# The low part of the SwiGLU and convolution weight tiles: GpSimd in place of VectorE

## The reference

```python
h = modulate(rmsnorm(x, norm_ffn[i]), sh2, sc2)
x = x + g2 * ((silu(h @ w_gate) * (h @ w_up)) @ w_down)      # D_FF = 2816
b, c, v = split(h @ w_in); y = (b * conv3(c * v)) @ w_out    # layer 1's mixer
```

## Time and profile before

| | |
|---|---|
| median of the runs | 2868.98 us |
| span of the profiled execution | 2866.1 us |
| TensorE matmuls, share of the span | 90% |
| VectorE | 1353.8 us, 47% |
| ScalarE | 672.1 us, 23% |
| GpSimd | 343.2 us, 12% |
| mean granted TensorE clock | 0.945 |
| `w_lo` on VectorE | 172 instructions, 203.1 us |

### The profile page before, as it was taken

One profiled execution on the slowest core, in us unless ns is written; L12 is line 12 of the kernel. 1 busy time (PEld: TensorE's weight loads), 2 busy tenths in 40 slices (PEclk: granted clock), 3 DMA queues, 4 the chain that ended last, 5 costly groups with the idle time before them and its releaser, 6 DMA issues.

```text
span 2866.1 us, 30876 instructions
## 1 busy us (share of the span) xinstructions
PE 2585.1 (90%) x11501; PEld 2104.4 (73%) x11501; DVE 1353.8 (47%) x1995; ACT 672.1 (23%) x993; POOL 343.2 (12%) x241
## 2 busy tenths in 40 slices
PE   8658888888796999999999969999969999999997
PEld 8546667676584888888788747877748888888886
DVE  0645666666584444444444444334443334444334
ACT  2323444444433111111111231111221111111111
POOL 3322222222105000000000140000140000000002
PEclk9878999999997999999999969999969999999998
DMA  6000111111320222222222201111101111111101
GB/s 238 28 6 23 36 35 35 35 35 35 118 96 1 81 76 93 74 79 73 88 80 73 96 30 45 37 59 37 44 1 58 44 44 59 44 44 53 50 29 59
DMA packets 47978, 162.67 MB, mean 57 GB/s; under 512 B 5152, under 2 KB 6560, under 8 KB 47776
## 3 DMA queue, kind: packets, MB, share of 16 engines
q1 hardware_dynamic: 47904, 161.72, 16.6%
HBM read 157.51 MB, written 4.19 MB: 56 GB/s over the span
## 4 chain that ended last, share of the span: by engine, by line
PE 77%; DVE 7%; issue 7%; POOL 5%; ACT 3%; DMA 1%; DVEq 0%; ACTq 0%; SPq 0%; POOLq 0%
PE ps L315 23%; PE ps L316 22%; PE ps L317 22%; POOL tmp L1497 3%; POOL acc L1488 2%; PE ps L624 2%; PE ps L580 1%; PE ps L581 1%; PE ps L584 1%; PE ps L582 1%; ACT pbuf L921 1%; PE ps L585 1%; DVE w_lo L1094 1%; PE ps L494 1%; DVE pt_lo L1094 1%
## 5 line engine op out<-in xcount | busy, mean ns | idle before, releaser
L315 PE MATMUL ps<-h_hi,w_hi 128*128 128x512 f32 x1792 | 715.3, 399 | 78.1 <-DVE h_lo L1094 78.0
L316 PE MATMUL ps<-h_lo,w_hi 128*128 128x512 f32 x1792 | 708.1, 395 | 0.0
L317 PE MATMUL ps<-h_hi,w_lo 128*128 128x512 f32 x1792 | 707.9, 395 | 0.0
L315 PEld LDWEIGHTS ps<-h_hi,w_hi 128*128 128x128 f32 x1792 | 341.4, 191 | 173.8 <-DVE h_lo L1094 103.3
L1296 DVE SCALAR_TENSOR_TENSOR x<-ps,mods,x 128x512 f32<-128x512 f32 x480 | 350.2, 749 | 206.0 <-PE ps L317 204.5
L315 PE MATMUL ps<-g_hi,w_hi 128*128 128x512 f32 x960 | 382.1, 398 | 39.5 <-DVE x L1296 34.2
L317 PEld LDWEIGHTS ps<-h_hi,w_lo 128*128 128x128 f32 x1792 | 342.9, 191 | 72.6
L316 PEld LDWEIGHTS ps<-h_lo,w_hi 128*128 128x128 f32 x1792 | 343.3, 192 | 68.8
L316 PE MATMUL ps<-g_lo,w_hi 128*128 128x512 f32 x960 | 378.6, 394 | 0.0
L317 PE MATMUL ps<-g_hi,w_lo 128*128 128x512 f32 x960 | 377.9, 394 | 0.0
L1353 DVE TENSOR_TENSOR ab<-ab,ps 128x512 f32<-128x512 f32 x88 | 60.5, 688 | 634.6 <-PE ps L317 633.0
(11 more groups left out here) (168 smaller groups left out, 2703.0 us busy)
## 6 DMA issues: line engine op xcount, KB each, us to landing
raw<-stream SPq DMA_DIRECT2D x176, 512.0 KB, 4.2
mod_raw_f<-ada_rows SPq DMA_DIRECT2D x48, 512.0 KB, 3.4
mod_raw<-ada_rows SPq DMA_DIRECT2D x32, 512.0 KB, 3.5
ada_ring<-ada_pe SPq DMA_DIRECT2D x16, 512.0 KB, 13.0
x<-x_t SPq DMA_DIRECT2D x2, 2048.0 KB, 15.7
x<-x_t SPq DMA_DIRECT2D x8, 512.0 KB, 6.4
out_t<-x SPq DMA_DIRECT2D x16, 256.0 KB, 2.1
hraw<-head_w SPq DMA_DIRECT2D x8, 384.0 KB, 3.9
```

Of the source, the lines that this page charges most:

```text
L315: nc.tensor.matmul(out, w[0][wi], a[0][ai], start=start, stop=False)
L316: nc.tensor.matmul(out, w[0][wi], a[1][ai], start=False, stop=False)
L317: return nc.tensor.matmul(out, w[1][wi], a[0][ai], start=False, stop=stop)
```

## The change

From the first SwiGLU on, GpSimd makes every `w_lo`. VectorE's calls of `tile_lo` in `ffn_block`, `conv_block` and `turn` go, and GpSimd gets loops over the same tiles in the same order, with a wait for ScalarE's cast ahead of each. In the turn after the first SwiGLU the two down tiles come between GpSimd's multiplications for the two halves; in every phase GpSimd's tiles of the last block stand ahead of its sums of squares. Which tiles, buffers and slots are used, and what ScalarE, TensorE and SyncE do, stays. The 18 tiles made before the first SwiGLU stay on VectorE.

```diff
-        def ffn_block(blk, prefetch, mod_count, out_at, gate):
+        def ffn_block(blk, mod_count, out_at, gate):
             for f in range(2):
                 for half in range(2):
                     ffn_inner(blk, f, half)
                     share = mod_count // 4
                     mod_rows((2 * f + half) * share, (2 * f + half + 1) * share)
-                if prefetch:
-                    for k in range(2):
-                        tile_lo(w_lo[:, 2 * f + k, :], w_hi[:, 2 * f + k, :], k)
...
-                if prefetch:
-                    down_tiles()
...
         def conv_block(blk, col, gate):
-            for k in range(2):
-                tile_lo(w_lo[:, 6 + k, :], w_hi[:, 6 + k, :], k)
             for f in range(2):
...
                 conv_inner(blk, f, lambda tap: taps[:, tap:tap + 1])
-                for k in range(3):
-                    tile_lo(w_lo[:, 3 * f + k, :], w_hi[:, 3 * f + k, :], (3 * f + k) % 2)
...
+        def tile_lo(slot, k):
+
+            C.add("t_hi")
+            pool.wait_ge(t_hi, C.at("t_hi"))
+            nc.gpsimd.tensor_tensor(w_lo[:, slot, :], raw[k][:], w_hi[:, slot, :].bitcast(F32), ALU.subtract)\
+                .then_inc(t_lo, 1)
...
+        for p, (kind, blocks, _, _) in enumerate(PHASES[1:], 1):
+            if kind == "ffn":
+                with pool.Fori(0, blocks - 1) as i:
+                    C.enter(i, {"t_hi": 6})
+                    for k in range(6):
+                        tile_lo(k, k % 2)
+                    C.leave(blocks - 1)
+                if p < 3:
+                    for k in range(4):
+                        tile_lo(k, k % 2)
+            else:
+                with pool.Fori(0, blocks) as i:
+                    C.enter(i, {"t_hi": 8})
+                    for k in (6, 7, 0, 1, 2, 3, 4, 5):
+                        tile_lo(k, k % 2)
+                    C.leave(blocks)
+            if p < 3:
+                turn(p, down_tiles if kind == "ffn" else (lambda: None))
```

More of the change, by code:

```diff
@@ L1367, in mod_rows @@
                 C.add("mod_used")
-        def down_tiles():
-            for k in range(2):
-                tile_lo(w_lo[:, 4 + k, :], w_hi[:, 4 + k, :], k)
-        def ffn_block(blk, prefetch, mod_count, out_at, gate):
+        def ffn_block(blk, mod_count, out_at, gate):
             for f in range(2):
@@ L1435, in _ @@
             if kind == "ffn":
-                per = {"sil": 4, "pj": 8, "gm": 4, "t_hi": 6, "v": 4}
+                per = {"sil": 4, "pj": 8, "gm": 4, "v": 4}
                 if n_mod:
@@ L1440, in _ @@
                     C.enter(i, per)
-                    ffn_block(i + first_blk, True, n_mod, i * 4 + (N_PE_MOD + N_ATT_MOD), gate)
+                    ffn_block(i + first_blk, n_mod, i * 4 + (N_PE_MOD + N_ATT_MOD), gate)
                     C.leave(blocks - 1)
-                ffn_block(last, p < 3, 2 * n_mod, N_PE_MOD + N_ATT_MOD + n_mod * (blocks - 1), None)
+                ffn_block(last, 2 * n_mod, N_PE_MOD + N_ATT_MOD + n_mod * (blocks - 1), None)
             else:
@@ L1446, in _ @@
                 with dve.Fori(0, blocks - 1) as i:
-                    C.enter(i, {"t_hi": 8, "cs": 8, "zm": 4, "pj": 12, "v": 16})
+                    C.enter(i, {"cs": 8, "zm": 4, "pj": 12, "v": 16})
                     conv_block(i + first_blk, i * 6, gate)
@@ L1455, in _ @@
             if p < 3:
-                turn(last, job, gate, down_tiles if kind == "ffn" else (lambda: None))
+                turn(last, job, gate, lambda: None)
             else:
@@ L1562, in _, with turn @@
             group(gb, True)
-        for p in range(4):
+        def tile_lo(slot, k):
[3 more added lines that the diff above has]
+                .then_inc(t_lo, 1)
+        def turn(p, tail):
             j = J_MIX + 2 * p
@@ L1568, in _ @@
                 add_squares(j, m, HT)
[L1569 to L1572, removed]
             add_squares(j + 1, 1, HT)
@@ L1577, in _, with down_tiles @@
                     add_squares(j + 1, k + 2, HT)
+            tail()
             for k in range(KD):
                 mul_rstd(j + 1, x[:, k, HALF[1]], HT)
+        def down_tiles():
+            for k in range(2):
+                tile_lo(4 + k, k)
+        turn(0, lambda: None)
+        C.n["t_hi"] = PRO_TILES + N_OUT_TILES
+        pool.wait_ge(t_lo, PRO_TILES + N_OUT_TILES)
+        for p, (kind, blocks, _, _) in enumerate(PHASES[1:], 1):
[16 more added lines that the diff above has]
+                turn(p, down_tiles if kind == "ffn" else (lambda: None))
+        for j in (J_MIX + 6, J_MIX + 7):
+            for m in range(1, KD):
+                add_squares(j, m, HT)
 def kernel(x, c, ctx, c_ctx, ada_w, ada_b, norm_mix, norm_ffn, mla_w_dq, mla_q_norm, mla_w_uq, mla_w_dkv,
```

## The result

The kernel after takes 2904.99 us (median of 4 runs, 2903.16 to 2905.55), beside 2868.36 us for the kernel before on the same chip: 1.0131 times as long, with an interval of 1.0117 to 1.0146. The change costs 36.6 us where I had forecast 25. The sign, the places and nearly all the mechanisms are those of the forecast; the size of the clock's loss in the first SwiGLU is not, and the two turns lose more than it had.

The account below looks back on a forecast made before the run. TensorE, 90% busy, was taken as the bound, VectorE mattering only where TensorE waits for to_x. 22 + 20 + 2.2 + 1.1 - 20.3 = +25.0 on a span of 2866.1, plus 2.9 for the median: 2894.0 us, range 2861 to 2908.

Parts of the forecast that it names:

- One tile on GpSimd: A w_lo subtraction of 128x1024 on GpSimd takes 2.36 us, where VectorE needs 1.2.
- The port: VectorE and GpSimd share SBUF access; a blocked instruction waits for the other's whole instruction; to_x, reading PSUM, isn't held.
- a row product that isn't held: Faster rival, first SwiGLU: the row product passes beside GpSimd, -8 us, 2861 (2851 if the copy passes too); chance 0.17.
- The chain: First SwiGLU: VectorE's work from last up product (t) to to_x grows 2.2 us in ten blocks, +22 us.
- The clock: First SwiGLU: TensorE's clock halves after waits of 3.1 us, 2.0 us in each of ten blocks, +20 us.
- The last block: First SwiGLU's last block: two row products in the slot, to_x at 1636.2 for 1634.02, +2.2 us.
- The turn after it: Turn after the first SwiGLU: GpSimd's down tiles block the first of VectorE's diagonal scalings, +1.1 us.
- the 2 us that I had named as a sign: Sign in the turn after the first SwiGLU: diagonal scalings of about 2 us.
- The convolution: Convolution: to_x no longer waits for the third tile's load; three blocks regain 6.8 us each, -20.3 us.
- The fourth block: Convolution's last block: TensorE waits for GpSimd's sums in place of to_x; 0, between -1.3 and +1.4 us.
- The second SwiGLU: Second SwiGLU: g_lo ends at t + 4.0 and to_x follows, against t + 4.1 before; 0.
- the slowest rival: GpSimd keeps the port for both tiles; second SwiGLU waits too, convolution regains half: +50 us, 2919; chance 0.07.

Follow-up runs that it names:

- experiment 3: The kernel after with each GpSimd w_lo tile made by two instructions of 128x512: 2869.27 us, 1.0007 of the kernel before.
- experiment 7: The kernel after with the fourth row product of each looped first-SwiGLU block replaced by a one-column copy: 2869.83 us, 1.001 of the kernel before.
- experiment 6: The kernel before, all w_lo on VectorE, with tiles TensorE doesn't need yet moved behind the first two or eight to_x: 2834.47 us, 0.9889.
- experiment 4: The kernel before with two extra VectorE tile subtractions in the second slot of each looped first-SwiGLU block: 2920.94 us, 1.0188.
- experiments 1: The kernel after with the first SwiGLU's tiles on VectorE again: 2849.09 us, 0.9938 of the kernel before.
- experiment 2: The kernel after with GpSimd's second pair of tiles of each first-SwiGLU block behind the first to_x: 2838.82 us, 0.9903 of the kernel before.
- experiment 5: The kernel before with one extra VectorE tile subtraction in the second slot of each looped first-SwiGLU block: 2886.85 us, 1.007.

## Why the prediction was right, and where it was short

*One tile on GpSimd*: 2.36 taken, 2.40 measured for a tile alone. Right.

*The port.* Right in each step of the first SwiGLU: `g_lo` 2.90 (2.8 forecast), the row product 3.40 (3.4), `to_x` at t + 7.85 (t + 7.7, from 1032.8). The chance of 0.17 for a row product that isn't held was open only because no row showed the form beside GpSimd; it is held. The Trainium skill, "SBUF — State Buffer", section "Who interferes with whom", says that a VectorE instruction with two SBUF inputs contends with a GpSimd instruction that reads SBUF. The trace agrees (0.69 to 2.90, 1.22 to 3.40), and so it does in the other direction: `to_x`, which reads one input from PSUM, kept its 0.75. The same section of the Trainium skill names copies and scalings among what may contend, and experiments 3 and 7 agree with that for a copy of four elements (0.99 and 2.05 for 0.16). Another page of the Trainium skill, "Perfetto Trace Analysis", says in "Optimizing Scalar/DVE Operations" that offloading between these two engines might not help. The convolution's gain speaks against that as a general rule, though experiment 6 has the same gain without GpSimd; the first SwiGLU speaks for it.

*The chain*: 22 forecast, 23.6 measured (10 x 2.36).

*The clock*: 20 forecast, and this is the term that was mis-sized. A block became 71.64 - 66.48 = 5.2 us longer, of which 2.36 is the wait; 2.8 a block is left, 28 in ten. I had charged 2.0, from the excess of one convolution block. That block is of the kind with less of it. Here are the row of VectorE's timeline of before that starts the next block, and three stretches of before behind the two waits, which I had not read:

```profile
1962.56 2.06 DVE L1296 SCALAR_TENSOR_TENSOR x<-ps,mods,x 128x512 f32<-128x512 f32 x3
```
```profile
1774.90:1778.30 3.40, 3.33 (x8) 2.65 (x9) 2.46 (x5) 0.00 (x0) 0.00 (x0) 0.53 0.49 154
1778.30:1781.70 3.40, 3.40 (x16) 2.75 (x16) 1.77 (x3) 0.00 (x0) 0.00 (x0) 0.97 0.00 0
...
1872.20:1875.60 3.40, 3.40 (x12) 2.67 (x12) 1.03 (x2) 0.00 (x0) 0.00 (x0) 0.72 0.00 0
```

The block that I took (93.80) was back at 0.97 after 3.4 us; the next one (1962.56 - 1867.96 = 94.60) was still at 0.72 in its second stretch, and its excess is 94.60 - 87.04 - 4.8 = 2.8. The first SwiGLU's waits all came out like the second kind. The earlier trace rows had the first of its two stretches and not the second. The third interval (93.45) has an excess of only 1.6, so the mean of the three is 2.1: the convolution's blocks gave the spread, but nothing in them said that the first SwiGLU would have the high end of it every time. Experiment 4 shows that the 2.8 belongs to the wait and not to GpSimd: same wait, same 6.8 us at half clock, same block.

*The last block*: 2.2 forecast. By its `to_x` the kernel after is 54.6 us late, 0.7 of it from the start, ahead of any change. 53.9 less the 23.6 and the 28 leaves 2.3. Right.

*The turn after it*: 1.1 forecast, 2.9 measured. VectorE's diagonal scalings and GpSimd's two down tiles:

```profile
1742.82 1.66 DVE L1104 TENSOR_SCALAR diag<-ident,rr 128x128 f32<-128x128 f32 x4
...
1739.07 4.74 POOL L1556 TENSOR_TENSOR w_lo<-raw,w_hi 128x1024 fp32r<-128x1024 f32 x2 [1.86 <-ACT w_hi L803]
```

The four take 1.66 for 0.88, the first of them 1.08 and not the 2 us that I had named as a sign; and GpSimd's multiplication behind them comes 1.2 later, counted from their start. That is near the 1.1 worked out, but in part by luck: the held scaling is 0.8 of it, and the other 0.4 lies in TensorE's broadcast, half of which ran at half clock. The remaining 1.6 I had no term for. By the trace's clock records the clock is halved between the last block's first `to_x` and the end of this turn for 61.4 us after and 54.6 before, which may be it; no experiment took that apart.

*The convolution*: -20.3 forecast for three blocks, -20.2 measured (261.7 us for 281.9). The fourth block was put at 0 and gave -0.7, inside its range: GpSimd's third tile is followed by its sums at once, and TensorE waits 5.5 us for them where it waited 4.8 for `to_x` before. TensorE's waits of after in 1700 to 2120, which hold none for `to_x`:

```profile
PE ps L315 <- DVE h_lo L1094: 26.0, 15, 4.3
PE ps L474 <- POOL acc L1475: 5.5, 1, 5.5
```

The turn behind it, another 1.6 late, had no term either, and the tiles alone don't make it. From the convolution's last product with `h` to the last up product of the next block it takes 120.1 us before and 120.9 after; the kernels of experiments 1 and 2 run the same code there as after and take 119.2 and 121.0. What makes the difference stays open.

*The second SwiGLU*: 0 and 0. GpSimd never kept the port for both tiles, so the slowest rival falls.

The sum in the profiled executions: 53.9 + 2.9 - 20.9 + 1.6 + 0.7 = 38.2, the difference of the spans. Of the 13 us beyond my 25.0, some 8 are the clock, 1.6 the chain, and 3.4 the two turns; 0.7 is the start, and the fourth convolution block gives 0.7 back. The medians differ by 36.6. The forecast of 2894.0 lies 11 us under the 2905 measured, which is inside the range, near its upper end: its own terms reach that with a clock cost between the 2.0 taken and the 3.4 given as the end. In part that is luck: the room that the range kept for the clock also had to hold 5 us of chain and turns that had no room of their own.

## What to carry to other kernels

Before an instruction goes from VectorE to GpSimd, list what VectorE does in the same microseconds between the last input and the next thing that TensorE waits for. Each instruction there with two SBUF inputs, and small copies too, can be made to wait for a whole GpSimd instruction, so 2.4 us of work taken off the chain made it 2.4 us longer, while `to_x`, which reads PSUM, ran beside the same tiles at its old 0.75. And read a chain for order first: moving the tiles behind the first `to_x` on the same engine gained 33 us against the kernel before on its chip, beside 27 for the best share of GpSimd (experiment 2), a difference that their intervals don't settle, and both are well ahead of the plain move. When one excess stands for a cost that recurs, look at all its neighbours in the trace and let the range span them: 93.80, 94.60 and 93.45 lay side by side.

## What the runs showed of the hardware that I had not expected

- A VectorE copy of 128x4 fp32 took 0.99 and 2.05 us beside a GpSimd subtraction, and of the eight copies of 128x3 in the convolution (0.16 each before) four took 2.36 and one 0.93 after the change; a copy of 128x1 beside GpSimd took 0.14 (experiment 7). Taking a held instruction away doesn't shorten the chain by what it took: its 3.40 us gave 1.38, as the copy was held in its place (experiment 7).
- The cost of a wait is not proportional to its length. 0.9 us left the clock alone in ten of ten blocks; 1.9 and 2.2 us halved it in five and four of ten, for 3.4 us each, 1.6 us a block; 3.3 us halved it in all ten, for 6.8 us, 2.8 us a block. So one more subtraction of 1.2 us ahead of `to_x` in ten blocks cost 19.7 us (experiment 5, medians), and a second one 35.1 more (experiment 4).
- Nor does the length alone decide. Waits of 1.9 us halved the clock and left it alone by turns, with halved tiles (experiment 3) and with whole ones (7); and in the convolution of before, waits of 4.8 us were followed by half clock for 3.4 us twice and for 6.8 us twice. What decides between equal waits is not shown here.
